# Second attention: the logarithm ahead of a step's exponentials, and VectorE's small operations between the two maps

## What is computed

```python
def _diff_attention(q, k, v, lam, lam_init, subln_g, slopes):
    ...
        scores = jnp.einsum('bqhmd,bshmd->bhmqs', qblk, k).astype(jnp.float32) * scale
        ...
        scores = scores - slopes[:, None, None, None] * delta.astype(jnp.float32)
        scores = jnp.where(delta >= 0, scores, NEG_INF)
        p = jax.nn.softmax(scores, axis=-1)
        a = p[:, :, 0] - lam * p[:, :, 1]
        return jnp.einsum('bhqs,bshe->bqhe', a.astype(v.dtype), v)
    ...
    out = _rmsnorm(out, subln_g) * (1.0 - lam_init)
```

## Time and profile before

| | |
|---|---|
| time, three runs | 2739.23 us median (2737.96 to 2741.26) |
| the profiled execution | 2738.89 us, span 2737.1 us |
| granted clock of PE, mean | 0.978 |
| PE busy | 2598.2 us, 95% of the span |
| DVE busy | 1531.7 us, 56% |
| ACT busy | 1109.5 us, 41% |
| POOL busy | 857.6 us, 31% |
| differential steps, start of the first to the end of the stage on PE | 1707.65 to 1851.84 us |

### The profile page before, as it was taken

One profiled execution on the slowest core, in us unless ns is written; L12 is line 12 of the kernel. 1 busy time (PEld: TensorE's weight loads), 2 busy tenths in 40 slices (PEclk: granted clock), 3 DMA queues, 4 the chain that ended last, 5 costly groups with the idle time before them and its releaser, 6 DMA issues.

```text
span 2737.1 us, 34710 instructions
## 1 busy us (share of the span) xinstructions
PE 2598.2 (95%) x12391; PEld 2161.8 (79%) x12391; DVE 1531.7 (56%) x2083; ACT 1109.5 (41%) x1865; POOL 857.6 (31%) x627
## 2 busy tenths in 40 slices
PE   6999999999899999999899988889997999999998
PEld 4888887788788899987688878668776888887887
DVE  5665665630424566657853438766578777771112
ACT  5200102511410688846544437661265555551000
POOL 2233331032232566620222220333101322325664
PEclk8999999999999999999999999999998999999999
DMA  6344444262455544434353346414242333338833
GB/s 242 100 142 136 143 134 123 77 222 86 146 197 168 126 111 109 112 119 154 103 176 115 109 149 169 152 32 169 85 131 93 102 115 108 108 106 306 288 94 122
DMA packets 377272, 374.81 MB, mean 137 GB/s; under 512 B 36323, under 2 KB 284556, under 8 KB 376972
## 3 DMA queue, kind: packets, MB, share of 16 engines
q1 hardware_dynamic: 346844, 303.91, 37.3%
q10 hardware_dynamic: 30256, 68.69, 6.7%
HBM read 286.55 MB, written 85.98 MB: 136 GB/s over the span
## 4 chain that ended last, share of the span: by engine, by line
PE 76%; DVE 12%; ACT 4%; DMA 3%; issue 1%; SPq 1%; POOL 1%; ACTq 0%; DVEq 0%; POOLq 0%
PE PS L1773 28%; PE PS L1861 20%; PE PS L1930 8%; PE PS L810 5%; PE PS L1820 3%; PE PS L788 2%; PE PS L2001 2%; DMA mod_raw<-in_w_ada 1%; PE PS L774 1%; PE PS L773 1%; DVE prob L1185 1%; PE PS L1843 1%; PE PS L1975 1%; DVE M L2659 1%; DVE Xr L2981 1%
## 5 line engine op out<-in xcount | busy, mean ns | idle before, releaser
L1773 PE MATMUL PS<-opA,w_hi 128*128 128x512 f32 x2176 | 680.2, 392 | 3.0 <-POOL w_lo L1579 3.0
L1773 PEld LDWEIGHTS PS<-opA,w_hi 128*128 128x128 f32 x2176 | 411.1, 189 | 89.3 <-POOL w_lo L1579 3.4
L1773 PE MATMUL PS<-opA,w_lo 128*128 128x512 f32 x1088 | 425.4, 391 | 0.0
L1574 POOL CAST w_hi<-w_raw 128x1024 fp32r<-128x1024 f32 (+1 forms) x117 | 123.4, 1055 | 793.2 <-PE PS L1773 448.2
L1861 PE MATMUL PS<-opB,Xr 128*128 128x512 f32 x1120 | 312.1, 396 | 17.4 <-ACT M L2324 17.4
L1579 POOL TENSOR_TENSOR w_lo<-w_raw,w_hi 128x1024 fp32r<-128x1024 f32 (+1 forms) x118 | 285.2, 2417 | 34.8 <-ACT w_hi L2203 25.4
L1861 PE MATMUL PS<-opA,Xr 128*128 128x512 f32 x980 | 277.2, 393 | 6.2 <-ACT M L2324 3.0
L1861 PEld LDWEIGHTS PS<-opB,Xr 128*128 128x128 f32 x1120 | 214.7, 192 | 64.2 <-ACT M L2324 18.6
L2659 DVE SCALAR_TENSOR_TENSOR M<-mod_raw,small,M 128x512 f32<-128x512 f32 x168 | 177.6, 1057 | 139.5 <-DMA mod_raw<-in_w_ada 80.4
L1773 PEld LDWEIGHTS PS<-opA,w_lo 128*128 128x128 f32 x1088 | 205.6, 189 | 42.4 <-issue 0.2
L1861 PEld LDWEIGHTS PS<-opA,Xr 128*128 128x128 f32 x980 | 183.0, 188 | 50.1 <-ACT M L2324 8.3
(11 more groups left out here) (266 smaller groups left out, 4777.5 us busy)
## 6 DMA issues: line engine op xcount, KB each, us to landing
mod_raw<-in_w_ada SPq DMA_DIRECT2D x96, 256.0 KB, 2.9
z_dram<-opB ACTq DMA_DIRECT2D x44, 512.0 KB, 3.9
w_raw<-in_a_w_in SPq DMA_DIRECT2D x32, 512.0 KB, 4.5
hin<-q_dram SPq DMA_DIRECT2D x64, 256.0 KB, 6.0
w_raw<-in_w_down SPq DMA_DIRECT2D x32, 512.0 KB, 3.9
opA<-z_dram SPq DMA_DIRECT2D x60, 256.0 KB, 5.3
mod_raw<-in_b_mod_w SPq DMA_DIRECT2D x48, 256.0 KB, 2.9
X<-x_dram SPq DMA_DIRECT2D x24, 512.0 KB, 5.9
```

Of the source, the lines that this page charges most:

```text
L1574: pool.tensor_copy(hi, raw).then_inc(pool_done, 1)
L1773: ins = pe.matmul(ps, w[:, k0 + k, :], rhs(part, k0 + k), start=(k == 0 and n == 0), stop=(k == chunks - 1 and n == 2))
```

## The change

The logarithm of `factor` becomes a function of its own, `factor_ln`, and ACT executes it at the head of a step, ahead of the step's two exponentials; the rest, `factor_exp`, stays where `factor` stood.

On DVE the reciprocal leaves `combine` and is given between the two fused instructions of the next step (`combine_reciprocal`); for the last item it stands ahead of `combine`. The factor now waits for the reciprocal by name, and the combination for the factor by name. The fused instructions wait for everything given so far only for the first three items; in later ones, in a head's first step, for the scaled bias, and for the combination of the item three back (`PAIRS`), whose buffers they write. The reciprocal waits for ACT alone.

```diff
--- before.py
+++ after.py
@@ -1073,12 +1073,16 @@
                 act.activation(half_tile(h)[:, 0, :], PS[:, 6 + h % 2, :], ACT.Square).then_inc(act_done, 1)
                 step(act_done, "sec_sq", h)
 
-            def factor(h):
+            def factor_ln(h):
 
                 act.wait_ge(pe_done, at("sec_ss", h))
                 r = half_tile(h)[:, 0, :]
                 act.activation(r, PS[:, turn_bank(PLACE[None, h]), :], ACT.Ln, scale=1.0 / P).then_inc(act_done, 1)
                 step(act_done, "sec_ln", h)
+
+            def factor_exp(h):
+
+                r = half_tile(h)[:, 0, :]
                 act.wait_ge(act_done, at("sec_ln", h))
                 act.activation(r, r, ACT.Exp, scale=-0.5).then_inc(act_done, 1)
                 step(act_done, "sec_rr", h)
@@ -1091,10 +1095,12 @@
 
             for t in range(SECOND_STEPS):
                 x = turned_at(t)
+                if half_at(t, RMS_LAG) is not None:
+                    factor_ln(half_at(t, RMS_LAG))
                 if values_first(t) and t < STEPS:
                     rows_exp(t)
                 if half_at(t, RMS_LAG) is not None:
-                    factor(half_at(t, RMS_LAG))
+                    factor_exp(half_at(t, RMS_LAG))
                 if x is not None:
                     copies(x)
                 if t < SWA_STEPS:
@@ -1166,7 +1172,7 @@
                     dve.wait_ge(pool_done, at("bias_d"))
                     dve.wait_ge(dve_done, now(dve_done))
                     dve.tensor_scalar(bias[:, 0, :], bias[:, 0, :], 0.25, None, ALU.mult).then_inc(dve_done, 1)
-                    step(dve_done)
+                    step(dve_done, "bias_scaled", x)
                 for m in (1, 0):
                     bank = 2 * m + DIFF_BANK[x]
                     c = MX + x % 4 * 4 + m
@@ -1175,18 +1181,24 @@
                     dve.wait_ge(pe_done, at("sec_S", x, m))
                     if d >= PAIRS:
                         dve.wait_ge(pe_done, at("sec_T", last_piece(x - PAIRS)))
+                        dve.wait_ge(dve_done, at("sec_n", x - PAIRS))
                     elif d == 0:
                         dve.wait_ge(pe_done, at("sec_pv", SWA_STEPS // 2 - 1, 1))
                     else:
                         dve.wait_ge(pe_done, at("sec_T", last_piece(SWA_STEPS - 1)))
                         if d == 2:
                             dve.wait_ge(pe_done, at("sec_pv", SWA_STEPS - 1, 1))
-                    dve.wait_ge(dve_done, now(dve_done))
+                    if d < PAIRS:
+                        dve.wait_ge(dve_done, now(dve_done))
+                    elif d % NT == 0:
+                        dve.wait_ge(dve_done, at("bias_scaled", x))
                     dve.tensor_tensor_reduce(out=pair[(x - SWA_STEPS) % PAIRS][m][:, 0:w], in0=bias[:, 0, T - w:],
                                              in1=PS[:].rearrange("p b t -> p (b t)")[:, bank * HALF:bank * HALF + w],
                                              scale=1.0, scalar=-MASKED * 1e3, op0=ALU.add, op1=ALU.min,
                                              accum_out=small[:, c:c + 1]).then_inc(dve_done, 1)
                     step(dve_done, "sec_p", x, m)
+                    if m and x - 1 >= SWA_STEPS:
+                        combine_reciprocal(x - 1)
 
             def swa_norm(x):
                 c = x % 4 * 4
@@ -1204,19 +1216,21 @@
                     dve.tensor_scalar(p, p, r[:, b:b + 1], None, ALU.mult).then_inc(dve_done, 1)
                     step(dve_done, "sec_n", x)
 
+            def combine_reciprocal(x):
+                c = x % 4 * 4
+                dve.wait_ge(act_done, at("sec_e", x, 0))
+                dve.reciprocal(small[:, RI + c + 1:RI + c + 2], small[:, RS + c + 1:RS + c + 2]).then_inc(dve_done, 1)
+                step(dve_done, "sec_r", x)
+
             def combine(x):
                 c, w = x % 4 * 4, (diff_item(x)[1] + 1) * P
                 r, f = small[:, RI + c + 1:RI + c + 2], small[:, RI + c:RI + c + 1]
                 p0, p1 = (pair[(x - SWA_STEPS) % PAIRS][m][:, 0:w] for m in range(2))
-                dve.wait_ge(act_done, at("sec_e", x, 0))
-                dve.wait_ge(dve_done, now(dve_done))
-                dve.reciprocal(r, small[:, RS + c + 1:RS + c + 2]).then_inc(dve_done, 1)
-                step(dve_done)
-                dve.wait_ge(dve_done, now(dve_done))
+                dve.wait_ge(dve_done, at("sec_r", x))
                 dve.scalar_tensor_tensor(out=f, in0=r, scalar=small[:, LAMS:LAMS + 1], in1=small[:, RS + c:RS + c + 1],
                                          op0=ALU.mult, op1=ALU.mult).then_inc(dve_done, 1)
-                step(dve_done)
-                dve.wait_ge(dve_done, now(dve_done))
+                step(dve_done, "sec_f", x)
+                dve.wait_ge(dve_done, at("sec_f", x))
                 dve.scalar_tensor_tensor(out=p0, in0=p1, scalar=f, in1=p0, op0=ALU.mult, op1=ALU.add).then_inc(dve_done, 1)
                 step(dve_done, "sec_n", x)
 
@@ -1246,6 +1260,8 @@
                 if 0 <= t - 1 < SWA_STEPS:
                     swa_norm(t - 1)
                 elif t and t - 1 < STEPS:
+                    if t == STEPS:
+                        combine_reciprocal(t - 1)
                     combine(t - 1)
                 y = valued_at(t - 1)
                 if y is not None and y < SWA_STEPS and y % 4 >= 2:
```

## The result

The changed kernel takes 2716.7 us in the median of four runs (2713.57 to 2723.49), the kernel before 2740.24 us in the runs taken beside it. The ratio is 0.9915, with a 95% interval of 0.9901 to 0.9929, so it is 19 to 27 us faster. I had forecast 2724.1 us, in a range of 2718 to 2732.

The account below looks back on a forecast made before the run. Heads were taken as bound by chains from engine to engine, with DVE late from n=4 to n=6 and PE from n=0 to n=3. Savings of 3.1 + 4.2 + 5.3 + 3.5 - 1.0 = 15.1 us gave 2724.1 us, range 2718 to 2732.

Parts of the forecast that it names:

- the scaling of n=3: DVE's scaling of the bias at n=3 (a head's steps are n=0 to 7): 0.2 us ahead of before.
- the deduction for POOL: POOL's epsilon additions, twice a head, would hold DVE's factor of n=4: 1.0 us taken off in all.
- the first head: Steps n=4 to 7 at 0.72 us each and 0.25 ahead of them, no logarithm at n=6: 3.1 us saved.
- DVE's waits: Dropped same-engine waits and the moved reciprocal cut a width-896 step from 4.38 to 3.65 us; 0.72 used per step.
- The rule that waits are free anyway: Rival: DVE's gaps stay with or without waits, only the logarithm pays, 4.7 us, 2734.5 us; chance 0.10.
- The logarithm at n=6: Moved first, it shrinks PE's 2.72 us stop and takes DVE's 1.21 us idle at n=7 away; 1.04 counted.
- The logarithm at n=2: Exponentials held behind PE's column sum and the logarithm delay n=3's second fused operation, eating the tenths DVE won there.
- second head: Same 4.1 us as the fourth head's sum, and 0.1 from a start without a wait: 4.2 us saved.
- third head, with the clock: 4.1 us, and 1.2 more from PE's clock not falling behind the stop at n=6: 5.3 us saved.
- fourth head and end: PE passes its last wait 3.8 us earlier, then waits 0.3 us for copies: 3.5 us saved.
- PE or ACT takes over: Rival: copies and exponentials collide from n=4 to n=7, half of 0.72 per step lost, 2729.5 us; chance 0.16.
- Slower: Rival: the logarithm holding both exponentials for PE costs 5.9 us at n=2 and n=6, 2745 us; chance 0.04.

Follow-up runs that it names:

- x3: Kernel before with only DVE's waits changed; reciprocal at its old place, logarithm still behind the exponentials: ratio 0.9962, 2729.81 us.
- x4: Kernel before with only the reciprocal moved between the two fused instructions; every DVE instruction still waits for all before it: ratio 1.0001, 2739.87 us.
- x6: Changed kernel with the logarithm back behind the exponentials, plus eight unread PE products at n=6 of heads 2 to 4: ratio 0.9942, 2725.0 us.
- c_before: The kernel before, measured and traced once more, unchanged: 2738.53 us, ratio 1.0.
- x10: Changed kernel with POOL's two branch-weight subtractions moved from heads 2 and 3 into the first head's fifth and seventh step: ratio 0.9933, 2722.98 us.

## Why the prediction was right or wrong

The places and the mechanism were right; what failed is the sum of the stage, 15.1 us said and 19.5 measured. Its terms that were mis-sized: the scaling of n=3 (1.9 us too little), the deduction for POOL (1.0 taken off beside terms that held it already), the first head (1.0 too little: 0.85 us a step where I had 0.72, and 0.60 us ahead of n=4 where I had 0.25) and the stretch from n=4 to the last scaling of the other heads (0.5 too little).

**What bounds the kernel.** Right. DVE was the latest from n=4 to n=7, the stop on line 1080 was the one at n=6, and removing each shortened the heads. The gain arrived behind the stage: 19.5 to 22.3 us in the stage, 21.5 and 23.5 us in the medians.

**DVE's waits.** The mechanism was right, the term was mis-sized: 0.85 us a step instead of 0.72. Both uncertain terms came out at their lower bounds. Between the first read and the second fused instruction pass 0.08 us, not 0.16: I had taken the reciprocal's own duration, although showed other instructions starting before the one ahead had ended. From second read to combination pass 0.25 us, not 0.28. The combination to the next step took 1.20, as said (1.19). x3 and x4 show whose gain it is: the waits', with the reciprocal's place adding to it only behind them.

**The rule that waits are free anyway** would have given 2734.5 us. x3, which differs from the kernel before by these waits alone, takes 10 us off. The Trainium skill (VectorE: DVE Perf Modes, section The DRAIN you can't avoid) has the next operation wait for the empty pipe with or without a semaphore; the rows here disagree, 0.08 us from start to start behind a reciprocal of 0.16. They fit another section of that page, Two Vector instructions with no wait between them, by which an instruction that isn't held may start before the earlier ones are done.

**The logarithm at n=6.** Right in place, cause and price; the stop shrank to 0.25 us (said: under 0.5), and the step from n=6 to n=7 of the fourth head fell from 5.02 to 3.13 us, by 1.89: 0.85 for DVE's waits, as in the first head, and 1.04 for the stop. What the sum does not tell is how the gain divides. With DVE's change alone that step still takes 4.87 us (x6, fourth head), since DVE, being faster, waits longer for PE; so 0.7 us of its gain reach the end only with the logarithm moved, and the move is worth 1.05 us alone and 1.7 behind DVE's change. Neither is a term that the sum has wrong.

**The logarithm at n=2.** This was the largest error in the sum. I let it eat all of DVE's gain in three heads and counted 0.2 us at the scaling of n=3 (0.3 in the second head). The scaling, measured from the head's start, came 0.85 us earlier in the second head (11.97 to 11.12), 1.43 in the third (13.63 to 12.20) and 0.30 in the fourth (12.07 to 11.77). So the price was right for the fourth alone. In the other two POOL's subtraction, which I had found, delays DVE past it: it cost the third head 1.56 us before (the scaling at 13.63 against 12.07 in the fourth head) and 0.43 after, because it now runs beside ACT's wait; I had these rows and carried them as a separate cost, not as cover for this one. That is 1.9 us of the miss.

**POOL.** What I foresaw happened: the factor met the epsilon's addition in three heads, 0.61 us instead of 0.21, 1.2 us of DVE's time in all against the 1.0 that I took off. I missed the second meeting, at n=1, which takes 3.0 us of DVE's time in the three heads and hardly counts in the fourth, since DVE then waits for PE. And the terms from n=4 to the last scaling came out above mine with the first loss in them (3.81, 4.88 and 3.98 us against 3.65, 4.85 and 3.65), so a separate deduction was wrong. Whether the 0.4 us would reach the end of the head if POOL gave them back was not tried.

**The sum.**

| | said | measured | difference |
|---|---|---|---|
| first head | 3.1 | 4.1 | 1.0 |
| second head | 4.2 | 4.9 | 0.7 |
| third head, with the clock | 5.3 | 6.6 | 1.3 |
| fourth head and end | 3.5 | 3.9 | 0.4 |
| POOL | -1.0 | in the heads | 1.0 |
| stage | 15.1 | 19.5 | 4.4 |

The end gave back 0.67 us (18.38 to 19.05) where I said 0.6. The medians fell by 21.5 and 23.5 us, 2 to 4 us more than the stage of the first pair of traces. Up to 3 of it can be the fall of the clock ahead of the fourth head's end, which c_before shows and the trace that I read did not; the stops of n=6 had a fall behind them in 8 of 15 cases. The rest is within the spread of the runs.

**The other rivals.** "PE or ACT takes over" did not happen: no head lost half of the 0.72. "Slower" was priced on exponentials held at n=2; that mechanism exists and costs 0.7 us in one head.

## What to carry to other kernels

For the whole change, add what each step saves to the stall as it stands before; for one part alone, ask what the stall that stays will give back: here DVE's idle time grew from 1.21 to 1.65 us once DVE alone had become faster. Before a cost is added to a sum, look whether a delay already found at the same place covers it, and try the parts of a change alone and together. A wait for everything an engine was given so far is cheap to write, and here such waits cost 0.71 us in a step of seven instructions on a chain where that engine is the latest; name the instruction whose result is read instead, and then move small work into the gaps.

## What the runs showed of the hardware

A same-engine wait on DVE costs 0.25 us ahead of a fused instruction over 896 columns: 0.17 us idle, and the 0.08 us by which it otherwise overlaps the accumulator read. Ahead of a 128x1 factor it costs next to nothing, since 0.19 us passes from the reciprocal's start to the factor's, and the reciprocal alone lasts 0.16.

A DVE instruction with two SBUF inputs that starts beside a two-input one of POOL's ends behind it: the combination of width 1024 (1.28 us alone) 1.08 us later, that of width 256 (0.48) 0.28, the 128x1 factor (0.22) 0.02. What matters is not the hold but who is late when it comes: one subtraction cost 2.1 us in the first head of x10, where DVE is the latest, and 0.4 in the third of the changed kernel.

PE's granted clock fell from 2.4 to 1.2 GHz in this stage behind stops of 2.2 to 2.8 us, but not behind each (8 of 15 at n=6): the fourth head of the kernel before ran at 1.00 in one trace and at 0.89 in the next. In the first head a stop of 1.7 us was followed by slow scores in one trace of the changed kernel (3.75 us for eight) and not in the other (2.06). Products that nothing reads, put into the stop, went with 1.00 in the heads 2 to 4 of both kernels that had them, and made the kernel before faster (0.9981, 0.9972 to 0.999) while adding 2.1 us of work to each of three places.
